# Decay blocks of a gated delta rule: decay sums and key factors carried as rows through memory, in place of products and transposes on TensorE

## The reference

```python
g = jnp.cumsum(g.reshape(B, H, N, C), axis=-1)
kb = k * beta[..., None]
decay = jnp.exp(jnp.where(incl, g[..., :, None] - g[..., None, :], NEG_INF))
L = jnp.where(strict, jnp.einsum('bhnid,bhnjd->bhnij', kb, k) * decay, 0.0)
T = lax.linalg.triangular_solve(L + eye, eye, left_side=True, lower=True)
intra = jnp.where(incl, jnp.einsum('bhnid,bhnjd->bhnij', q, k) * decay, 0.0)
```

## Time and profile before

| | |
|---|---|
| median of 3 runs | 1199.94 us (1199.6 to 1199.96) |
| the profiled execution | 1200.0 us, of which the span from first to last instruction is 1198.2 us |
| TensorE products | busy 1188.3 us, 99% of the span |
| VectorE | 753.2 us, 63% |
| ScalarE | 609.4 us, 51% |
| GpSimd | 110.8 us, 9% |
| read from and written to memory | 220.35 MB and 4.72 MB |

### The profile page before, as it was taken

One profiled execution on the slowest core, in us unless ns is written; L12 is line 12 of the kernel. 1 busy time (PEld: TensorE's weight loads), 2 busy tenths in 40 slices (PEclk: granted clock), 3 DMA queues, 4 the chain that ended last, 5 costly groups with the idle time before them and its releaser, 6 DMA issues.

```text
span 1198.2 us, 16074 instructions
## 1 busy us (share of the span) xinstructions
PE 1188.3 (99%) x6330; PEld 992.3 (83%) x6330; DVE 753.2 (63%) x990; ACT 609.4 (51%) x895; POOL 110.8 (9%) x149
## 2 busy tenths in 40 slices
PE   9999999999999999999999999999999999999997
PEld 7899888888878888888888888888777778888886
DVE  5776977766575666556455554676665656676654
ACT  6656554644433456534434444574446446555443
POOL 0002020259700110000000000000000000000000
PEclk9999999999999999999999999999999999999999
DMA  8878776566744455555665686566556455454862
GB/s 290 259 207 249 207 198 192 165 207 182 205 135 139 143 163 149 179 187 171 207 192 188 193 293 197 184 199 221 202 187 217 158 193 176 126 156 151 297 195 96
DMA packets 145530, 229.24 MB, mean 191 GB/s; under 512 B 12658, under 2 KB 63538, under 8 KB 144432
## 3 DMA queue, kind: packets, MB, share of 16 engines
q1 hardware_dynamic: 142016, 214.59, 57.7%
q0 software_dynamic: 3120, 12.57, 3.3%
q10 hardware_dynamic: 320, 1.06, 0.2%
HBM read 220.35 MB, written 4.72 MB: 188 GB/s over the span
## 4 chain that ended last, share of the span: by engine, by line
PE 99%; DMA 0%; ACT 0%; DVE 0%; issue 0%; SPq 0%; POOLq 0%; POOL 0%; ACTq 0%
PE acc L2094 69%; PE acc L2084 10%; PE acc L2086 5%; PE aux L1973 4%; PE acc L2035 3%; PE aux L2283 1%; PE aux L2311 1%; PE acc L2425 1%; PE aux L2058 1%; PE aux L2172 1%; PE aux L2276 1%; PE aux L2304 1%; DMA raw_w<-in_w_in 0%; PE aux L2221 0%; PE aux L2213 0%; PE aux L2168 0%
## 5 line engine op out<-in xcount | busy, mean ns | idle before, releaser
L1406 DVE TENSOR_TENSOR lo_w<-raw_w,hi_w 128x1024 fp32r<-128x1024 f32 (+2 forms) x381 | 464.3, 1225 | 327.0 <-ACT hi_w L1002 325.3
L2094 PE MATMUL acc<-hi_w,h_both 128*128 128x512 f32 (+3 forms) x1800 | 559.5, 385 | 0.0
L1002 ACT ACTIVATE hi_w<-raw_w 128x1024 fp32r<-128x1024 f32 (+2 forms) x381 | 394.1, 1049 | 285.9 <-PE acc L2094 185.0
L2094 PEld LDWEIGHTS acc<-hi_w,h_both 128*128 128x128 f32 x1800 | 332.3, 188 | 67.6 <-issue 4.9
L2094 PE MATMUL acc<-lo_w,h_both 128*128 128x512 f32 (+3 forms) x900 | 341.1, 379 | 0.0
L2094 PEld LDWEIGHTS acc<-lo_w,h_both 128*128 128x128 f32 x900 | 169.4, 188 | 28.7
L2084 PE MATMUL acc<-h_both,hi_w 128*128 128x512 f32 x512 | 180.3, 397 | 0.0
L2086 PE MATMUL acc<-h_both,lo_w 128*128 128x256 f32 x512 | 142.9, 279 | 0.0
L2084 PEld LDWEIGHTS acc<-h_both,hi_w 128*128 128x128 f32 x512 | 96.1, 188 | 23.0
L2086 PEld LDWEIGHTS acc<-h_both,lo_w 128*128 128x128 f32 x512 | 96.4, 188 | 0.1
L2094 PE MATMUL acc<-hi_w,m_hi 128*128 128x512 f32 x224 | 87.7, 391 | 0.0
(11 more groups left out here) (355 smaller groups left out, 1177.8 us busy)
## 6 DMA issues: line engine op xcount, KB each, us to landing
raw_w<-in_w_in SPq DMA_DIRECT2D x275, 512.0 KB, 4.1
raw_w<-in_w_out SPq DMA_DIRECT2D x64, 512.0 KB, 4.7
raw_w<-in_w_branch_a SPq DMA_DIRECT2D x16, 512.0 KB, 4.6
raw_w<-in_w_branch_b SPq DMA_DIRECT2D x16, 512.0 KB, 4.8
raw_w<-in_cmp_k_w SPq DMA_DIRECT2D x8, 512.0 KB, 6.2
raw_w<-in_cmp_v_w SPq DMA_DIRECT2D x8, 512.0 KB, 6.2
raw_w<-in_w_in SPq DMA_DIRECT2D x8, 384.0 KB, 4.6
x_in<-in_x SPq DMA_DIRECT2D x8, 256.0 KB, 7.3
```

The lines of the kernel that those rows point to most:

```text
L1002: act.activation(piece_flat(hi_w[slot], no), piece_flat(raw_w[no % RAW_SLOTS], no), ACT.Copy).then_inc(*hi_ready.event(no))
L1406: dve.tensor_tensor(piece_flat(lo_w[slot], no), piece_flat(raw_w[no % RAW_SLOTS], no), piece_flat(hi_w[slot], no).bitcast(F32), ALU.subtra ...
L2094: i = pe.matmul(to[:, t, 0:group.cols], x[at], w[:, k], start=first and k == 0 and m == 0, stop=last and k == n - 1 and m == 2)
```

## The change

The running sum of g and the key factors `k_low` reach the partitions as rows by way of memory, and VectorE makes the turned block itself.

- `g_rows` (GpSimd, tick 34, ahead of `v_shift(0)` in the list): writes `gcum` (128 x 16) turned into a small tensor in memory, waits until that has landed, and reads it back with the same 2048 numbers on every partition (`g_row`, 1 MB).
- `k_rows(h)` (GpSimd, ticks 53 and 57): the same for `k_low` of a half of the heads, in two transfers each way (2 x 512 numbers there, 2 x 256 KB back, into `k_row`).
- `gu`, the two products with `ones_r` and `tri_flip` are gone, with what they need (`g_hi`, `g_lo`, `ones_r`).
- `decay` reads `g_row` in SBUF, no longer waits for `gram`, and stands a tick earlier, ahead of `z_out(1)` in tick 66.
- `tri` has two more multiplications: the key block in PSUM by the masked decay, then by `k_row`, into `low_t`.

```diff
--- before
+++ after
@@ -221,11 +221,13 @@
     at(10, "r1_row")
     at(10, "z_out", 0)
 
-    at(18, "ones_r")
     for n, step in enumerate(("ba", "softplus", "gates", "gcum", "exp_gcum")):
         at(END[("conv", "v", 0, 0)] + 1 + n, step)
+    at(END[("conv", "v", 0, 0)] + 5, "g_rows")
     for h in range(2):
         at(conv_end("k", h) + (13, 8)[h], "k_scale", h)
+    at(conv_end("v", 0) + V_TICKS[0][-1] + 1, "k_rows", 0)
+    at(conv_end("k", 1) + 8, "k_rows", 1)
 
     for h in range(2):
         for part in "qk":
...
@@ -251,11 +253,9 @@
     for h in range(2):
         for t in range(NT):
             s = base + 4 * (NT * h + t)
-            at(s, "gu", h, t)
             at(s + 1, "gram", h, t)
-            at(s + 2, "decay", h, t)
+            at(s + 1, "decay", h, t)
             at(s + 3, "tri", h, t)
-            at(s + 5, "tri_flip", h, t)
             at(s + 5, "blocks_away", h, t)
     at(base + 18, "solve")
     base += 46
...
@@ -531,8 +528,8 @@
         attn_t = arena("attn_t", [P, HEADS, NT, P], F32, 40)
         chain = [{n: arena(f"{n}{t}", [P, QUAD, P], F32, 48 + 8 * t + 2 * i)
                   for i, n in enumerate(("low_m", "inv", "wide"))} for t in range(NT)]
-        gu_hi, gu_lo = ([arena(f"gu_{n}{t}", [P, QUAD, P], F32R, 48 + 8 * t + kb) for t in range(NT)]
-                        for n, kb in (("hi", 4), ("lo", 2)))
+        g_row = arena("g_row", [P, NT, HEADS, P], F32, 100)
+        k_row = arena("k_row", [P, NT, HEADS, P], F32, 64)
         low_t = [[arena(f"low_t{h}{t}", [P, QUAD, P], F32, (54 + 8 * t, 96 + 2 * t)[h]) for t in range(NT)]
                  for h in range(2)]
         small_block = arena("small_block", [2 * NT * 4 * QUAD, BLOCK, BLOCK], F32, 100)
...
@@ -890,6 +891,29 @@
                     pool.dma_start(block_scratch[0][b, t, quad(h)].rearrange("i r c -> r i c"),
                                    diagonal_block(chain[t]["wide"], b)).then_inc(*blocks_out[h][t].event(b))
 
+            def g_rows():
+
+                pool.wait_ge(*dve_did.after("gcum"))
+                pool.dma_start(g_scratch.rearrange("n p -> p n"), gcum, allow_slow_non_contiguous=True).then_inc(
+                    *g_away.event(0))
+                pool.wait_ge(*g_away.after(0))
+                pool.dma_start(g_row[:].rearrange("p t h c -> p (t h c)"),
+                               g_scratch.rearrange("n p -> (n p)").partition_broadcast(P)).then_inc(*g_back.event(0))
+
+            def k_rows(h):
+
+                pool.wait_ge(*pool_did.after("k_scale", h))
+                rows = [slice(t * HEADS + h * QUAD, t * HEADS + (h + 1) * QUAD) for t in range(NT)]
+                for t in range(NT):
+                    pool.dma_start(k_scratch[rows[t]].rearrange("n p -> p n"), k_low[:, rows[t]],
+                                   allow_slow_non_contiguous=True).then_inc(*k_away[h].event(t))
+                pool.wait_ge(*k_away[h].after(NT - 1))
+                pool.wait_ge(*dve_did.after("v_tap", 0, 6))
+                for t in range(NT):
+                    pool.dma_start(k_row[:, t, quad(h)].rearrange("p h c -> p (h c)"),
+                                   k_scratch[rows[t]].rearrange("n p -> (n p)").partition_broadcast(P)).then_inc(
+                        *k_back[h].event(t))
+
             def v_shift(h):
 
                 pool.wait_ge(*act_did.after("v_raw", h, 1))
...
@@ -1081,6 +1103,7 @@
                 act.wait_ge(*used.after(c))
                 if (part, h, s) == ("q", 0, 0):
                     act.wait_ge(*dve_did.after("v_tap", 1, 6))
+                    act.wait_ge(*dve_did.after("tri", 1, 1))
                 act.activation(m_t[part][:, two(h, s)], pairs_of(c)[:, :, 1], ACT.Copy).then_inc(
                     *act_did.event("half", "moba", part, h, s))
 
...
@@ -1127,18 +1150,17 @@
             def decay(h, t):
 
                 c = chain[t]
-                act.wait_ge(*pe_did.after("gram", h, t))
+                if h:
+                    act.wait_ge(*dve_did.after("tri", 0, t))
+                elif t == 0:
+                    act.wait_ge(*g_back.after(0))
+                    act.wait_ge(*dve_did.after("ssq", "k", 1))
                 for i in range(QUAD):
                     o = t * HEADS + h * QUAD + i
-                    last = act.activation(c["inv"][:, i], aux[:, 0, i * P:(i + 1) * P], ACT.Abs,
+                    last = act.activation(c["inv"][:, i], g_row[:, t, h * QUAD + i], ACT.Abs,
                                           bias=ngcum[:, o:o + 1])
                 link(last)
                 act.activation(c["inv"][:], c["inv"][:], ACT.Exp, scale=-1.0).then_inc(*act_did.event("decay", h, t))
-
-            def tri_flip(h, t):
-                act.wait_ge(*pe_did.after("tri_flip", h, t))
-                act.activation(low_t[h][t][:], aux[:, 3].rearrange("p (i c) -> p i c", c=P), ACT.Copy).then_inc(
-                    *act_did.event("tri_flip", h, t))
 
             def delta(h, n):
                 bank_to = {0: (0, delta_u), 1: (1, delta_s), 3: (1, delta_u)}
...
@@ -1444,9 +1466,6 @@
                 link(dve.tensor_scalar(sp0, sp0, -1.0, None, ALU.mult))
                 dve.tensor_tensor(tiles(g, HEADS), tiles(sp0, HEADS), over_heads(nexp, NT), ALU.mult).then_inc(
                     *dve_did.event("g"))
-                dve.wait_ge(*dve_did.after("g"))
-                link(dve.tensor_copy(g_hi[:], g))
-                dve.tensor_tensor(g_lo, g, g_hi[:].bitcast(F32), ALU.subtract).then_inc(*dve_did.event("g_parts"))
 
             def gcum_():
                 dve.wait_ge(*pe_did.after("gcum"))
...
@@ -1552,22 +1571,14 @@
                 to = (q_ssq if part == "q" else k_ssq)[h]
                 dve.tensor_reduce(tiles(to, QUAD), sq[:], AXX, ALU.add).then_inc(*dve_did.event("ssq", part, h))
 
-            def gu(h, t):
-                o = t * HEADS + h * QUAD
-                if (h, t) == (0, 0):
-                    dve.wait_ge(*dve_did.after("g_parts"))
-                    dve.wait_ge(*pe_did.after("conv_back", "k", 1))
-                    dve.wait_ge(*act_did.after("silu", "k", 1))
-                if h:
-                    dve.wait_ge(*blocks_out[0][t].after(3))
-                    dve.wait_ge(*act_did.after("tri_flip", 0, t))
-                for to, part in ((gu_hi[t], g_hi[:].bitcast(F32)), (gu_lo[t], g_lo)):
-                    last = dve.tensor_tensor(to[:], over_heads(upto[:]), over_cols(part[:, o:o + QUAD]), ALU.mult)
-                last.then_inc(*dve_did.event("gu", h, t))
-
             def tri(h, t):
                 c = chain[t]
                 dve.wait_ge(*act_did.after("decay", h, t))
+                dve.wait_ge(*pe_did.after("gram", h, t))
+                if h:
+                    dve.wait_ge(*blocks_out[0][t].after(3))
+                if t == 0:
+                    dve.wait_ge(*k_back[h].after(NT - 1))
                 dve.tensor_tensor(c["low_m"][:], c["inv"][:], over_heads(below[:]), ALU.mult)
                 link(dve.tensor_tensor(low_t[h][t][:], c["inv"][:], over_heads(upto[:]), ALU.mult))
                 if t == 0:
...
@@ -1579,14 +1590,18 @@
                     last = dve.scalar_tensor_tensor(c["wide"][:, i], aux[:, 1, i * P:(i + 1) * P], k_low[:, o:o + 1],
                                                     c["low_m"][:, i], ALU.mult, ALU.mult)
                 last.then_inc(*dve_did.event("tri", h, t))
+                dve.wait_ge(*dve_did.after("tri", h, t))
+                link(dve.tensor_tensor(low_t[h][t][:], aux[:, 1].rearrange("p (i c) -> p i c", c=P), low_t[h][t][:],
+                                       ALU.mult))
+                dve.tensor_tensor(low_t[h][t][:], low_t[h][t][:], k_row[:, t, quad(h)],
+                                  ALU.mult).then_inc(*dve_did.event("tri_turned", h, t))
 
             def lift(h, t):
 
                 inv_q = inv_t[:, quad(h), t]
                 if (h, t) == (0, 0):
+                    dve.wait_ge(*dve_did.after("tri_turned", 1, 1))
                     dve.wait_ge(*blocks_back.after(3, NT - 1))
-                    for t_ in range(NT):
-                        dve.wait_ge(*act_did.after("tri_flip", 1, t_))
                 link(dve.tensor_tensor(inv_q, inv_q, over_heads(upto[:]), ALU.mult))
                 dve.transpose(chain[t]["inv"][:], inv_q).then_inc(*dve_did.event("lift", h, t))
 
...
@@ -2157,27 +2172,15 @@
                 last.then_inc(*pe_did.event("conv_back", part, h))
 
             def gram(h, t):
-                take(0, (act_did, "decay", h, t))
-                pe.wait_ge(*act_did.after("ones_r"))
-                take(1, (dve_did, "tri", h, t))
+                take(1, (dve_did, "tri_turned", h, t))
                 take(2, (dve_did, "tri", h, t))
-                pe.wait_ge(*dve_did.after("gu", h, t))
                 for part in "qk":
                     pe.wait_ge(*act_did.after("silu", part, h))
-                for m, part in enumerate((gu_hi[t], gu_lo[t])):
```

(26 more changed lines are left out.)

## The result

The changed kernel takes **1221.66 us** (median of 4 runs, 1220.29 to 1222.57) against 1199.95 before: a ratio of 1.0181 (95% interval 1.0163 to 1.0198), 21.7 us slower. Forecast were 1196.2 us and a range up to 1204.0. The profiled execution took 1222.57 us.

What follows compares the result with a forecast made beforehand. TensorE's own instruction list, busy 99% of the span, was taken as the bound. The 1200.0 us of the profiled execution less 3.85 for dropped instructions, plus 0 for hidden transfers, gave 1196.2 us, with a range up to 1204.

Steps and rivals of the forecast that it cites:

- What leaves TensorE: Two products with ones_r (2.09 us) and four transposes of wide each turn (1.76 us) leave TensorE's list: 3.85 us less.
- the cover of ScalarE's table loads and VectorE's blocks: Weight halves start some 8.2 us before TensorE wants them, so two 1.28 us table loads and VectorE's swapped multiplications cost nothing.
- L: In g_rows, tick 34: time until the 2048 4-byte pieces have landed in memory, taken as 6.0 us, between 4.0 and 8.1.
- The second rival: Scatter goes piece by piece at 9.2 ns, L is 19.4 us, TensorE waits 13 us at piece 43: 1212 us, chance 0.16.
- B: In g_rows: time the 1 MB broadcast back to all partitions moves, taken as 4.0 us, between 3.4 and 7.9.
- L + B + 115.95: Time in us when the first shift of v lands behind scatter and broadcast; forecast 125.95, against 126.4 allowed.
- The limit of 10.5 for L + B: At piece 43, TensorE stays covered while scatter landing plus broadcast take under 10.5 us.
- The second chain: k_rows, ticks 53 and 57: two scatters taken as 4.0 us, VectorE's wait ends at 188.4 against 191.1: hidden.
- the third rival: Another engine or the weight stream becomes late, another 0.5 MB delaying piece 66's weight load: 1197 to 1201 us, chance 0.07.

Runs made afterwards that it cites:

- experiment 6: Changed kernel with rows moved behind the shifts of v and numbers turned on VectorE, written in 128-byte pieces: 1195.84 us, ratio 0.9968 to the kernel before.
- experiment 2: Changed kernel, order kept, with sums and factors written to memory as they lie, in 128 long pieces (rows come back permuted): 1200.69 us, ratio 1.0014 to before.
- experiments 4 and 5: Changed kernel with products of constants put into TensorE's two waits: 95 and 64 of them 1231.55 us, 50 and 35 of them 1218.38 us.
- experiment 1: Changed kernel with g_rows and k_rows(1) moved behind the shifts of v, pieces still 4 bytes: 1198.7 us, ratio 0.9994 to the kernel before.

## Why the prediction was wrong

- **What leaves TensorE: right.** 3.85 us were forecast, 4.05 measured without transfers (95% interval of the ratio: 2.5 to 5.3 us). That the cover of ScalarE's table loads and VectorE's blocks holds was right as well: there and in experiment 6 TensorE waits for neither.
- **L failed, the step that decided.** It was taken as 6.0 us from `inv_t`, "as the row nearest in number of pieces", with 8.1 as the upper end; measured 13.1. The row had the number but not the size or direction of the pieces: 128 bytes out of memory, here 4 bytes into it. The second rival's 9.2 ns a piece, and 19.4 us, were too much; 5.8 ns fit. Of the 3.5 us from which it took 9.2 ns, some 1.65 were the issues of three more transfers (3 x 0.55), read as time of pieces; without them 4.8 ns come out. The Trainium skill, weighed in the prediction, had the sign: "DMA: Bandwidth & Descriptors", Rules for kernel authors, one descriptor per element and the advice to rearrange. Experiments 2 and 6 agree with it. The Trainium skill's fixed 2.0 us for a transfer plus bytes over 436 GB/s ("DMA: Bandwidth & Descriptors", Anatomy of one DMA) agrees with the 128 pieces (1.9 us) and not with the 2048 (13.1); there the measurement decides.
- **B was too small, but did not decide.** Taken as 4.0, with 7.9 as the upper end; the shift was done at 138.81, which by the sum's own form (L + B + 115.95, 1.7 us added as the sums came at 105.69 and not at 104.00) makes L + B 21.2, and B about 7.7 with L at 13.4, issue to wake. The limit of 10.5 for L + B was good: 21.2 is 10.7 past it, and TensorE waited 11.3. In experiment 2 the shift was done at 124.3; the same form makes L + B 8.4 there, with L at 2.3 and B at 6.1. That is under the limit, and TensorE does not wait at piece 43: the error in B alone would have stayed hidden. With L at 13.4 the limit is passed by 6.9 us even with the 4.0 of the forecast.
- **The second chain failed by the same price.** 4.0 us were taken for two scatters, 5.2 as the high end; 12.0 measured, and TensorE waited 7.9 where 0.4 was the most in the forecast's own bounds.
- **Two terms were missing.** The half clock behind a wait (5.7 us, experiments 4 and 5) stood in no case's sum, the rivals' with waits included. And the pieces were priced as a delay of their own chain; that they hold the weight stream at 29 to 40 GB/s was not foreseen (the third rival thought of bytes, another 0.5 MB). By itself it shows in the 2.9 us by which experiment 1 stays behind experiment 6.
- **The chances.** The second rival, at 0.16 and 1212, was the mechanism that came true; with the half clock it would have said some 1218. Part of that is luck: its piece was too dear, and its second site (3 us of waiting; 7.9 measured) too cheap. The forecast left it outside the range because the price of a piece was read from a row that was like it in one respect only.

## What to carry to other kernels

When a transfer's shape is not in the trace, price it by pieces and by their size, and let the worst nearby price into the range. A wait on a queue that feeds the critical path costs what stands behind it: put the new step behind, and turn short columns into runs on an engine with time to spare before they go to memory. And add to a forecast wait of TensorE what it costs afterwards: 3.0 and 2.7 us at half clock here, behind waits of 11.3 and 7.9.

## Not expected of the hardware

- Pieces of 4 bytes slow other queues down far beyond their own bytes: 8 KB held the whole core to 29 to 40 GB/s for about 9 us from GpSimd's queue, and to 5 to 35 GB/s for as long from ScalarE's. The kernel before moved 246 to 352 GB/s from 110 to 119 us.
- The profile's page counts them only on one of the two. In the change, ScalarE's queue (q10) shows 320 packets, and with the scatter on it

```profile
q10 hardware_dynamic: 2384, 1.07, 0.3%
```

2064 more, as many as the 2048 pieces and 16. GpSimd's queue (q0) has 3760 packets with 4096 short pieces (2048 of the sums, 4 x 512 of the factors) and 3744 with long ones: there a scatter can't be seen in the packets, only in its landing and in the GB/s of its stretch.
